# Key and value steps in twos, the sample's top-k between the prompt's rounds, 30 value steps beside the xl and gate products

## The reference, cut to what matters

```python
q, k = _rope(q, pos), _rope(k, pos)
lru, hT, new_buf = _rglru(xl, conv_buf, h0, conv_w, conv_b, w_a, b_a, w_i, b_i, lam)
att = attend(q, k, v, qi, ki, wi)          # prompt: top 128 of up to 512 keys a query; sample: top 256 of 2052
mix = concatenate([lru * gelu(gate), att]) @ w_out
x = x + _rmsnorm(mix, g_post_mix)
f = square(relu(_rmsnorm(x, g_pre_ffn) @ w_ff1)) @ w_ff2
```

## Time and profile before

| what | value |
|---|---|
| median of 3 runs | 829.79 us (828.88 to 830.25) |
| profiled execution | 829.45 us, span of its instructions 827.6 us |
| PE busy | 783.4 us, 95% of the span |
| DVE, ACT, POOL busy | 491.2, 435.9, 99.9 us |
| granted TensorE clock, mean | 0.987 |
| transferred | 166.89 MB, mean 202 GB/s over the span |

### The profile page before, as it was taken

How to read it: one execution, slowest core, us unless ns; L and a number is a source line. 1 busy time by engine, 2 the same in 40 slices (tenths; PEclk the granted TensorE clock), 3 DMA queues, 4 the chain that set the end, 5 groups by cost and what they waited for, 6 DMA issues and landing times.

```text
span 827.6 us, 16947 instructions
## 1 busy us (share of the span) xinstructions
PE 783.4 (95%) x6187; PEld 654.9 (79%) x6187; DVE 491.2 (59%) x966; ACT 435.9 (53%) x877; POOL 99.9 (12%) x113
## 2 busy tenths in 40 slices
PE   5996999999999988999989999999999999999993
PEld 3872577745876653468879999999999999999993
DVE  6307999998564436721668786444446755544444
ACT  3447655512386575642457787533337777643440
POOL 0787453400000010000000000000000100000000
PEclk8999999999999999999999999999999999999997
DMA  8445429999729999561215555555555655555541
GB/s 317 143 126 181 147 103 354 389 394 373 252 94 359 320 333 394 159 223 42 76 59 174 177 177 171 169 172 176 177 178 178 213 173 177 176 178 176 169 163 54
DMA packets 69791, 166.89 MB, mean 202 GB/s; under 512 B 8995, under 2 KB 14628, under 8 KB 69348
## 3 DMA queue, kind: packets, MB, share of 16 engines
q1 hardware_dynamic: 64484, 145.54, 51.7%
q10 hardware_dynamic: 2592, 10.59, 3.6%
q0 software_dynamic: 2656, 9.98, 3.3%
HBM read 161.40 MB, written 4.67 MB: 201 GB/s over the span
## 4 chain that ended last, share of the span: by engine, by line
PE 87%; ACT 4%; DVE 4%; DMA 3%; issue 1%; SPq 1%; DVEq 0%; ACTq 0%
PE bank L1797 47%; PE bank L1383 18%; PE bank L1616 5%; PE bank L1486 3%; PE bank L1592 3%; PE bank L1521 3%; DVE scp L1023 1%; PE bank L1714 1%; DMA regQ<-in_ck 1%; DMA regX<-in_cv 1%; PE bank L1726 1%; PE bank L1459 1%; PE bank L1500 1%; PE bank L1739 1%; PE bank L1369 1%
## 5 line engine op out<-in xcount | busy, mean ns | idle before, releaser
L1265 DVE TENSOR_TENSOR w_lo<-w_raw,w_hi 128x1024 fp32r<-128x1024 f32 x128 | 156.7, 1225 | 120.3 <-ACT w_hi L865 119.6
L865 ACT CAST w_hi<-w_raw 128x1024 fp32r<-128x1024 f32 x128 | 133.9, 1048 | 90.0 <-DMA w_raw<-in_w_mlp 90.0
L1797 PE MATMUL bank<-hn_hi,w_hi 128*128 128x272 f32 x512 | 147.9, 289 | 2.9 <-issue 2.9
L1797 PE MATMUL bank<-h_lo,w_hi 128*128 128x272 f32 x512 | 148.4, 290 | 0.0
L1797 PE MATMUL bank<-hn_hi,w_lo 128*128 128x272 f32 x512 | 148.2, 289 | 0.0
L1797 PE MATMUL bank<-h_hi,w_hi 128*128 128x272 f32 x512 | 147.8, 289 | 0.0
L1797 PE MATMUL bank<-h_hi,w_lo 128*128 128x272 f32 x512 | 147.6, 288 | 0.0
L1797 PE MATMUL bank<-hn_lo,w_hi 128*128 128x272 f32 x512 | 147.1, 287 | 0.0
L1797 PEld LDWEIGHTS bank<-hn_hi,w_hi 128*128 128x128 f32 x512 | 96.3, 188 | 3.4 <-issue 3.3
L1383 PE MATMUL bank<-regR,wring 128*128 128x272 f32 x384 | 94.9, 405 | 3.2 <-DVE regR L970 3.2
L1797 PEld LDWEIGHTS bank<-hn_lo,w_hi 128*128 128x128 f32 x512 | 96.5, 188 | 0.1
(11 more groups left out here) (253 smaller groups left out, 1191.6 us busy)
## 6 DMA issues: line engine op xcount, KB each, us to landing
w_raw<-in_w_mlp SPq DMA_DIRECT2D x128, 512.0 KB, 3.5
arena<-in_ck SPq DMA_DIRECT2D x96, 256.0 KB, 5.0
arena<-in_cv SPq DMA_DIRECT2D x96, 256.0 KB, 4.3
regQ<-in_ck SPq DMA_DIRECT2D x32, 256.0 KB
regX<-in_cv SPq DMA_DIRECT2D x32, 256.0 KB, 4.0
wring<-in_w_in ACTq DMA_DIRECT2D x12, 512.0 KB, 6.1
wring<-in_w_in SPq DMA_DIRECT2D x8, 512.0 KB, 8.2
regX<-in_xT SPq DMA_DIRECT2D x4, 544.0 KB, 5.6
```

The lines of the kernel that those rows point to most:

```text
L865: nc.scalar.copy(w_hi[n % 4][:, :], w_raw[n % 4][:, :]).then_inc(w_hi_rd, 1)
L1265: vec.tensor_tensor(w_lo[n % 4][:, :], w_raw[n % 4][:, :], w_hi[n % 4][:, :].bitcast(F32), ALU.subtract).then_inc(w_lo_rd, 1)
L1797: ins = pe.matmul(out, lhs[s][:, k * P:(k + 1) * P], rhs(k), start=(first and k == 0 and i == 0), stop=(last and k == KT - 1 and i == 2))
```

## The change

The prompt's top-k is copied to where xl will be. DVE does five of its rounds first, then the whole top-k of the sample, then the other eleven rounds, between which stand the masked adds of group 0; the mask follows. On PE the key steps and value steps come two at a time; the new keys' scores and the masks of group 0 stand inside the value product, on two banks of their own, and the masks of group 1 share one bank, one after every second pair of values in the xl product. The transposes of group 0 start in the first xl tile, and 30 value steps stand in the xl and gate stage, 2 in attention. In attention, scores, values and transposes go by pairs. The second half of the output weights is loaded by POOL behind the last value step. ACT's list is reordered to match.

```diff
-MID_VALUES = 19
+MID_VALUES = 30
+EARLY_ROUNDS = 5
...
+        mask_bank = [bank[6 + n % 2] if n < 5 else bank[5] for n in range(10)]
...
-        work_p = arena[:, at:at + 1152]
...
+        wp = {n: xl[:, QB - 1 - n, 3:3 + P * (n + 1)] for n in range(1, QB)}
...
             eng.wait_ge(v_mm, KSTEPS)
+            for m in range(CT, KT):
+                eng.dma_start(wring[:, 1, (m - CT) * PIECE:(m - CT + 1) * PIECE], w_out_d[m]).then_inc(out_in[m], 16)
...
-            eng.wait_ge(pmask_rd, 1)
             value_out(0)
...
+                if i == 2:
+                    for g in range(GRP):
+                        eng.wait_ge(kn_mm, g + 1)
+                        nc.scalar.mul(S[:, g, PAST:NKEY], bank[6 + g][:, 0:NS], SCALE).then_inc(kn_ev, 1)
+                elif i == 4:
+                    sample_exponentials(0)
+                    round_weights(XL, 0)
+                    round_weights(XL, 1)
...
+            for n in range(4):
+                sample_transposed(n)
+            eng.wait_ge(pmask_rd, 1)
             recurrent_half(0, 0)
...
+            prompt_rounds(0, EARLY_ROUNDS)
...
+            prompt_rounds(EARLY_ROUNDS, 11)
+            sample_masked(0)
+            sample_masked(1)
+            prompt_rounds(11, 12)
+            sample_masked(2)
+            sample_masked(3)
+            prompt_rounds(12, 13)
+            sample_masked(4)
+            sample_largest(0)
+            prompt_rounds(13, TOPK_P // 8)
+            prompt_masks()
             rest_of_weights(0)
...
+                if u == 20:
+                    sample_out(1)
...
+                    half_product(K, E_K, hf, m)
+                    two_key_scores(4 * m - 2 + 2 * hf)
...
+                    if j < 4 and k == 3:
+                        two_key_scores(10 + 4 * i)
+                        if i == 2:
+                            new_key_scores()
+                        elif i == 3:
+                            masks(2, 3)
+                if j < 4:
+                    two_key_scores(12 + 4 * i)
...
+                if i == 2:
+                    masks(0, 1)
+                elif i == 3:
+                    masks(4)
...
+            rounded_part(0)
+            two_key_scores(30)
+            two_transposes(0)
+            rounded_part(1)
+            two_transposes(2)
+            rest_part(0)
+            rest_part(1)
+            sample_transposes(4)
+            two_values(0)
+
+            split_half(XL, E_XL, 1, 0)
             two_gates(0, 0)
...
+            two_values(2)
+            masks(5)
+            split_half(XL, E_XL, 1, 1, lambda: two_gates(0, 2))
+            two_values(4)
+            masks(6)
+            split_half(XL, E_XL, 2, 0)
+            two_values(6)
+            masks(7)
+            split_half(XL, E_XL, 2, 1, lambda: two_gates(1, 0))
+            two_gates(1, 2)
+            two_values(8)
+            masks(8)
...
+            split_half(GATE, E_GATE, 0, 0, lambda: sample_transposes(5))
+            two_values(14)
+            sample_transposes(6)
+            two_gates(2, 2)
+            split_half(GATE, E_GATE, 0, 1, lambda: sample_transposes(7))
+            two_transposes(8)
+            two_values(16)
...
+            split_half(GATE, E_GATE, 3, 1)
+            two_values(28)
...
+            for w_ in range(ATT_UNITS // 2 + 2):
+                if w_ < ATT_UNITS // 2:
+                    att_scores(w_)
+                if w_ >= 2:
+                    att_values(w_ - 2)
+                if MID_VALUES + w_ < KSTEPS:
+                    value_products(MID_VALUES + w_)
+                if 1 <= w_ <= ATT_UNITS // 2:
+                    att_transposes(2 * w_ - 2)
+                    att_transposes(2 * w_ - 1)
...
+                        eng.wait_ge(pa_oe, ATT_UNITS // 2)
                         sample_out_transposes()
```

More of the change, by code:

```diff
@@ L308, in build @@
         xc_rd = sem("xc_rd")
-        out_in = [sem(f"out_in{m}") for m in range(CT)]
+        out_in = [sem(f"out_in{m}") for m in range(KT)]
         scan_rd = sem("scan_rd")
@@ L583, in rotary_tile @@
                     last.then_inc(gemm_ev, 1)
[L584 removed]
+                    if scores is not None:
+                        sample_scores(scores + 2 * hf)
                         sample_scores(scores + 2 * hf + 1)
@@ L1508, in _, with new_key_scores, sample_mask, masks @@
             half_product(K, E_K, 1, 0)
-            key_scores(0)
+            two_key_scores(0)
             for m in range(1, CT):
                 for hf in range(2):
-                    s = 4 * m - 3 + 2 * hf
-                    half_product(K, E_K, hf, m, lambda: key_scores(s))
-                    key_scores(s + 1)
+                    half_product(K, E_K, hf, m)
+                    two_key_scores(4 * m - 2 + 2 * hf)
+            def new_key_scores():
+                eng.wait_ge(rope_out, 13)
+                for g in range(GRP):
+                    for m in range(CT):
+                        for b4 in range(4):
+                            ins = pe.matmul(bank[6 + g][32 * b4:32 * b4 + 32, 0:NS], qbd[:, 4 * g + b4, m, :], kT[:, m, SEQ:NT],
+                                            start=(m == 0), stop=(m == CT - 1))
+                    ins.then_inc(kn_mm, 1)
+            def sample_mask(n):
+                g, c = n // 5, n % 5
+                cols = slice(c * 512, min((c + 1) * 512, NKEY))
+                if n == 0:
+                    eng.wait_ge(smask_rd, 1)
+                    eng.wait_ge(kn_ev, GRP)
+                elif n == 5:
+                    eng.wait_ge(k_ev, KSTEPS)
+                elif n > 5:
+                    eng.wait_ge(sm_ev, n)
+                elif n >= 2:
+                    eng.wait_ge(sm_ev, n - 1)
+                rows = slice(NS * min(c, 3), NS * min(c, 3) + NS)
+                taken = smask[rows, 0:CHUNK] if c < 4 else smask[rows, CHUNK:ROW]
+                pe.matmul(mask_bank[n][:, 0:cols.stop - cols.start], ind_r[rows, g, :], taken, start=True, stop=True).then_inc(sm_mm, 1)
+            def masks(*ns):
+                for n in ns:
+                    sample_mask(n)
             def value_tile(i):
@@ L1538, in _ @@
                 value_tile(i)
[L1540 to L1548, removed]
-            def sample_mask(n):
-                g, c = n // 5, n % 5
-                cols = slice(c * 512, min((c + 1) * 512, NKEY))
-                if n == 0:
-                    eng.wait_ge(smask_rd, 1)
-                    eng.wait_ge(kn_ev, GRP)
-                elif n >= 2:
-                    eng.wait_ge(sm_ev, n - 1)
-                rows = slice(NS * min(c, 3), NS * min(c, 3) + NS)
-                taken = smask[rows, 0:CHUNK] if c < 4 else smask[rows, CHUNK:ROW]
-                pe.matmul(bank[4 + n % 2][:, 0:cols.stop - cols.start], ind_r[rows, g, :], taken, start=True, stop=True).then_inc(sm_mm, 1)
             def sample_transposes(n):
```

243 lines of the change are left out of this document (99 added, 144 removed).

## The result

The changed kernel takes 844.12 us (median of 4 runs, 842.91 to 844.76) against 829.34 us (827.82 to 830.25): a ratio of 1.0161 with a 95% interval of 1.0137 to 1.0185, in which the plain quotient of the two medians, 1.0178, lies too. The medians differ by 14.8 us; the kernel is slower, and outside the forecast range of 820 to 834.5. The profiled execution took 844.76 us, with a span of 842.9 us and a mean granted clock of 0.976 (before: 827.6 us, 0.987).

A forecast was written before the change was run, and what follows sets the result against it. TensorE, busy 95% of the span, was taken as the bound: xl start at 210.8, plus a 100.4 us stage and 49.15 us of attention, ended attention 1.9 us earlier, so 829.45 - 1.9 = 827.5 us, range 820 to 834.5.

The forecast's parts named there:

- The step that failed: Attention's first four pairs: two value steps instead of four, but value 31 comes 1 to 2 us late; costed at 0.
- the forecast term: Attention: 49.15 us instead of 56.65, mainly because most value steps move out of it.
- 27 more steps take 71 us from value 3 on: Value loads: 27 steps of 1.05 MB at 398 GB/s, done about 300 to 302 with the gate weights, before PE wants them.
- one of the signs that the prediction named for being wrong: Xl and gate stage: PE waiting for value pages in the gate stage would show the forecast wrong; no size given.
- The start of the xl products: PE's first xl product: at 210.8 us instead of 211.88, set by DVE's list, bounds 209.1 and 212.5.
- The stage: Xl and gate stage: 100.4 us instead of 93.7, so attention starts at 311.2, 5.6 us later.
- a break: Xl and gate stage: breaking a product in the middle costs PE 0.23 us; eight fewer broken halves give -1.8.
- single breaks that cost nothing: PE's products: a sign for being wrong, since each break was priced at 0.23 us.
- The half-speed stretch: Attention near 319 us, granted clock 0.50 before the change: gone or not, costed at -0.8 us.
- the loads costed at nothing: Second half of the output weights, moved to POOL's queue: no cost; up to 5 us if its cover went.
- The slower one: Attention's first eight pairs: thinned of value steps, PE falls to 1.2 GHz, +9 us, 834.5 us in all; chance 0.23.
- Rival 4: Xl and gate stage: loads or ACT's chain hold it, each value moved out is paid by waits, 829.5 us; chance 0.10.

The follow-up runs named there:

- e5: e2 with the first rest of the weights ahead of the prompt's mask on VectorE: 830.14 us (0.9997).
- e11: The changed kernel with each value step fetching only two of its four pages, TensorE's instructions unchanged: 830.92 us (1.0014).
- e2: The changed kernel with value steps 30 and 31 behind the scores of pairs 4 and 6, not 0 and 1: 832.92 us (1.0036).
- e3: The changed kernel with both the edit of e1 and the edit of e2: 833.75 us (1.0046).
- e1: The changed kernel with POOL loading the first half of the output weights only behind the last value step: 837.23 us (1.0079).
- e14: e5 with attention in the order of before and edits shortening the stops at group 1's transposes: 830.32 us (0.9997).
- e15: e2 with seven instead of five of the prompt's rounds ahead of the sample's top-k: 833.67 us (1.0058).

## Why the prediction was wrong

**The step that failed** is in attention's first four pairs: "value 31, issued when step 27 is done and competing with the first half of the output weights, is 1 to 2 us late: 0". Place, cause and competitor were right; the size was not. It came 8.4 us late, PE has one list and stood still with it, and the half clock that followed stretched the pairs behind. Attention took 62.6 us instead of 49.15. Where the step doesn't wait and the clock holds (e5: 48.7), or its pages are half (e11: 49.5), the rest of the forecast term is right.

Behind the size stands the sentence that 27 more steps take 71 us from value 3 on, so that pages lie ready by 302. Value 3 was issued at 223.95, near 221 as forecast once the late start is added. But a step's pages are asked for only when the step four before is done: they follow PE's pace, not the DMA engines'. From 276 to 282, where PE stops, the DMA share is 0.38. So the last pages could not be issued before step 27 was done at 307.7; they were issued from 312.15 on, and the chain's 10.98 us follows from there. Twenty-seven steps at full rate were a price for a stream that never runs ahead. PE had waited for step 29's pages (0.47) at the end of the gate stage already, one of the signs that the prediction named for being wrong.

**The start of the xl products**, 210.8 with bounds to 212.5, came at 213.62. DVE's waits for the masks were 0.79 and 1.46 us, within the bounds. What was outside them is the sample's top-k on DVE: costed at 68.5 from before, it took 71.1 at its new place. e5 shows the late start to be worth 2.8 us where value 31 doesn't hold PE.

**The stage** came out right, 99.8 against 100.4, and 100.1 in e11, without waits for pages. The pairs cost 1.85 to 1.94, about as taken. But the agreement is in part luck. Three profiles with the same instructions in this stage took 102.9 (e2), 103.0 (e3) and 104.2 us (e1): the clock fell to about 0.5 from 213 to 215 behind the wait at the start in e2 and e3, and behind the stops at the transposes in e1, and after it did neither. Nor is each term right. The 2 us that PE should wait for the gates of block 1 did not come, and a break isn't worth 0.23 everywhere. From the chain of waits after:

```profile
284.69 1.85 PE bank L1633 x16
286.54 1.71 PE bank L1653 x12
288.25 0.92 PE bank L1528 x4
289.16 1.50 PE bank L1653 x12
290.66 1.85 PE bank L1633 x16
292.51 3.21 PE bank L1653 x24
```

The half that gate products break takes 1.71 + 1.50 = 3.21 us, as much as the whole one. The 0.2 us come with the first twelve products behind a value step (1.71 against 1.50 behind gates), and the six halves that stay broken hold only gates or transposes. So single breaks that cost nothing, another sign named for being wrong, do appear. The Trainium skill (TensorE: Matmul & The Clock Gate, Part 2: What happens when you issue a matmul) says that weight loads are pulled ahead of running matmuls; read as the prediction read it, this would have made the stage 104.4. The rows agree for gates and not for value steps, and after e1's 104.2 the length alone can't decide it.

**The half-speed stretch**, costed at -0.8, went the other way: it lasts from about 318 to 342, where before it lasted some 3.4 us from 318.8 on.

**Behind attention** nothing was costed, and 1.5 us were lost: after the stop of 2.85 us at the MLP's start, which is in both kernels, the clock fell. It does so in some executions of either order and not in others (last section), so nothing shows it to be an effect of the change. No wait for the loads costed at nothing shows.

**The rivals.** The slower one had the right sign and named the link, "a late value 31 empties PE first", but its price came from thinness alone; a fall of the clock without that link costs about 2 us (e2, e3). Rival 4, that loads hold the stage, isn't borne out: PE waits 0.47 us for pages in it, and with half the pages it takes as long (e11, 100.1). The loads took back the gain behind the stage, in attention.

**Left open**: e5's profile ends attention at 360.08, within 0.3 us of the forecast, and e14's span, 825.4 us, is within 0.3 of the forecast 825.7, though that profile is the fastest of e14's 12 executions. Yet their medians equal before's. In e5's profile 2.8 us are lost behind attention, with the clock at 0.50 where before's profile has 1.00. That this is what holds the medians fits, but wasn't shown.

## What to carry to other kernels

When a stream with few slots is used at a faster pace, price its last transfer from its own issue (slot free, issuer free) and not from the rate of a stream that runs ahead, and list every transfer that another queue issues in the same microseconds. A step whose data comes last should stand where the engine has other work in front of it: moving the last two value steps four and five pairs later (e2) was worth 11 us, where all of the reordering had promised 1.9. And an instruction's price is that of its old neighbours: in a new place it can stand beside another engine's work and take three times as long.

## What the runs showed of the hardware

**VectorE beside GpSimd.** Grouped instructions of DVE in the sample part (count, busy us, mean ns), after:

```profile
L1095 DVE SCALAR_TENSOR_TENSOR regM<-regM 32x256 f32<-32x256 f32 x1 | 1.5, 1452 | 0.0
L1082 DVE COPY regM<-top 32x256 f32<-32x256 f32 x3 | 1.3, 426 | 0.1
L1103 DVE TENSOR_SCALAR arena<-arena,least 128x544 f32<-128x544 f32 x1 | 1.6, 1615 | 0.0
```

GpSimd has a product running beside each of them (starts 159.69, 150.36 and 162.60). The same three before took 411, 282 and 497 ns, with no product beside them. The difference, 1.04 + 0.43 + 1.12 = 2.6 us, is all that the part grew by. In e15, with the part 6 us later, these three are short and others are long, DVE first, then GpSimd's products (timelines of the two engines):

```profile
160.37 0.41 DVE L1091 TENSOR_TENSOR regM<-regM 32x256 f32<-32x256 f32 x1
160.71 1.57 DVE L1092 TENSOR_TENSOR regM<-regM 32x256 f32<-32x256 f32 x1
162.32 1.45 DVE L1091 TENSOR_TENSOR regM<-regM 32x256 f32<-32x256 f32 x1
163.69 1.54 DVE L1092 TENSOR_TENSOR regM<-regM 32x256 f32<-32x256 f32 x1
165.27 0.41 DVE L1091 TENSOR_TENSOR regM<-regM 32x256 f32<-32x256 f32 x1
```
```profile
160.58 1.42 POOL L491 TENSOR_TENSOR lx<-lx 128x544 f32<-128x544 f32 x1 [7.88 <-ACT lx L582]
161.96 1.53 POOL L492 TENSOR_TENSOR lx<-lx 128x544 f32<-128x544 f32 x1
163.57 1.39 POOL L493 TENSOR_TENSOR arena<-lx 128x544 f32<-128x544 f32 x1
```

Beside each of GpSimd's three products one short DVE instruction lasts until 0.3 us after the product's end. The 64 `max` and `match_replace` instructions keep their means (728 and 709 ns) in both kernels, though products stand beside some of them too. The Trainium skill (SBUF — State Buffer, SBUF: two separate sides) says that VectorE and GpSimd contend for a shared pair of ports when the VectorE instruction runs in a two-port mode, or has two inputs in SBUF while the GpSimd one reads SBUF; the one that starts first holds the ports for its whole instruction and the other blocks. The rows agree for the instructions with two inputs; in which mode the copies and L1103 ran isn't shown.

**The clock after the same stop.** PE stops for about 2.85 us before the MLP in every profile. The windows behind it, before first, then e5:

```profile
426.00:428.00 2.00, 2.00 (x17) 2.00 (x17) 1.93 (x4) 0.00 (x0) 0.00 (x0) 1.00 0.00 0
```
```profile
424.00:426.00 2.00, 2.00 (x10) 2.00 (x10) 1.93 (x5) 0.00 (x0) 0.00 (x0) 0.50 0.00 0
426.00:430.00 4.00, 4.00 (x19) 3.84 (x18) 1.14 (x2) 0.43 (x2) 0.00 (x0) 0.53 0.00 0
```

The same stop is followed by 2.4 GHz in one execution and by 1.2 GHz in another. In six of the 19 profiles the clock stays at 1.00 behind it, and the stretch from attention's end to the last instruction takes 465.3 to 465.4 us; in eleven it is at 0.50 for some 3 to 4 us (466.7 to 467.0), in two for about 6 (468.1). Profiles with the order of before are among both the first and the second.
